# Narrow TensorE products placed among wide ones in a hybrid decoder block

## The reference, cut to what matters

```python
mod = (silu(c) @ ada_w + ada_b).reshape(B, 6, D)       # shift1, scale1, gate1, shift2, scale2, gate2
h = rms_norm(x, norm1_g) * (1 + scale1) + shift1
u = h @ w_in          # g_q, g_k, g_v, g_r, g_lr (16 wide, low rank), d_q, d_k, d_v, gate_a, gate_b
log_a = log_sigmoid(g_lr @ alpha_up + alpha_b) / 16    # per token, 4 heads x 64
# GLA in chunks of 64 tokens, for each chunk:
b = cumsum(log_a)                                      # forward sums
q_in, k_in = q * exp(b), k * exp(-b)
k_out = k * exp(b_last - b)                            # sums to the chunk's end
decay = exp(b_last)                                    # one number per chunk and channel: chunk sums
o_b = diff_attention(...)                              # d_q, d_k, d_v
x = x + gate1 * ((sig(gate_a) * (o_a @ w_a) + sig(gate_b) * (o_b @ w_b)) @ w_out)
h2 = rms_norm(x, norm2_g) * (1 + scale2) + shift2
x = x + gate2 * moe(h2)
```

## Time and profile before

| | |
|---|---|
| median of 3 runs | 1588.11 us (1584.22 to 1591.04) |
| profiled execution, its own time | 1586.0 us |
| its span, first to last instruction | 1584.2 us |
| TensorE busy | 1501.9 us, 95% of the span |
| VectorE, ScalarE, GpSimd busy | 520.9, 342.0 and 106.5 us |
| mean granted TensorE clock | 0.977 of full speed |

### The profile page before, as it was taken

The page is one execution under the profiler, slowest core; times in us unless marked ns, Lnnn a source line. Parts: engine busy times, 40 slices in busy tenths (PEclk is TensorE's granted clock), DMA queues, the critical chain, the costliest instruction groups (busy, mean ns, idle before and its releaser), DMA issues.

```text
span 1584.2 us, 20243 instructions
## 1 busy us (share of the span) xinstructions
PE 1501.9 (95%) x7989; PEld 675.8 (43%) x7989; DVE 520.9 (33%) x1074; ACT 342.0 (22%) x662; POOL 106.5 (7%) x140
## 2 busy tenths in 40 slices
PE   2999999999999999999999999889999899989896
PEld 2444545454545555444444455433333233323232
DVE  6576332323233224732222344652111111111010
ACT  4312322323233614211111112211101101101010
POOL 1000000000000000000000001001111111111101
PEclk9999999999999999999999999989999999999999
DMA  9760101010101011011130752469999999999982
GB/s 373 277 263 12 50 0 54 1 47 6 26 13 27 13 27 27 27 40 40 40 119 0 305 185 94 178 249 345 410 408 406 410 409 409 408 414 407 417 360 54
DMA packets 68748, 291.23 MB, mean 184 GB/s; under 512 B 12180, under 2 KB 36927, under 8 KB 53311
## 3 DMA queue, kind: packets, MB, share of 16 engines
q1 hardware_dynamic: 62096, 273.38, 43.5%
q0 software_dynamic: 6576, 16.79, 4.2%
HBM read 276.36 MB, written 20.07 MB: 187 GB/s over the span
## 4 chain that ended last, share of the span: by engine, by line
PE 86%; DMA 11%; DVE 2%; issue 1%; ACT 1%; SPq 0%; POOL 0%; POOLq 0%; ACTq 0%; DVEq 0%
PE PS L676 81%; DMA WK<-in_expert_w 5%; DMA R<-in_expert_w 3%; DMA R<-in_ada_w 1%; DMA out_rows<-R 1%; PE PS L1119 1%; PE PS L784 1%; PE PS L1141 1%; DVE R L1526 1%; PE PS L745 0%; ACT R L1216 0%; PE PS L1039 0%; PE PS L897 0%; DMA R<-in_x 0%; DVE R L1518 0%
## 5 line engine op out<-in xcount | busy, mean ns | idle before, releaser
L676 PE MATMUL PS<-R 128*32 128x512 f32 (+5 forms) x4058 | 747.1, 578 | 23.7 <-DMA R<-in_expert_w 7.5
L676 PEld LDWEIGHTS PS<-R 128*32 128x32 f32 (+4 forms) x4058 | 262.7, 129 | 396.8 <-issue 381.6
L676 PE MATMUL PS<-R,HT 128*128 128x512 f32 (+1 forms) x768 | 341.1, 599 | 3.7 <-DVE HT L1523 3.0
L676 PE MATMUL PS<-HT,R 128*32 128x512 f32 (+2 forms) x1184 | 314.4, 602 | 3.5 <-DMA WK<-in_expert_w 1.9
L1518 DVE TENSOR_TENSOR R<-R,PS 128x512 f32<-128x512 f32 (+1 forms) x95 | 71.6, 771 | 464.1 <-PE PS L676 464.1
L676 PEld LDWEIGHTS PS<-R,HT 128*128 128x128 f32 x768 | 143.9, 192 | 169.5 <-issue 168.1
L676 PEld LDWEIGHTS PS<-HT,R 128*32 128x32 f32 (+1 forms) x1184 | 105.8, 133 | 145.9 <-issue 143.1
L1216 ACT ACTIVATE R<-PS 128x512 f32<-128x512 f32 (+4 forms) x129 | 76.8, 605 | 396.9 <-PE PS L676 252.7
L676 PE MATMUL PS<-WK,R 128*32 128x512 f32 (+1 forms) x384 | 95.2, 614 | 4.5 <-DMA R<-in_expert_w 4.5
L640 POOL DMA_INDIRECT out_rows<-R x37 | 53.6, 1448 | 309.1 <-DVE R L1526 172.8
L1216 ACT ACTIVATE R<-PS,S,A 128x128 f32<-128x128 f32 x88 | 33.1, 456 | 189.5 <-PE PS L1119 189.5
(11 more groups left out here) (239 smaller groups left out, 831.4 us busy)
## 6 DMA issues: line engine op xcount, KB each, us to landing
R<-in_expert_w SPq DMA_DIRECT2D x67, 2048.0 KB, 34.9
HT<-in_expert_w SPq DMA_DIRECT2D x20, 2048.0 KB, 32.8
R<-in_ada_w SPq DMA_DIRECT2D x24, 1024.0 KB, 7.4
WK<-in_expert_w SPq DMA_DIRECT2D x9, 2048.0 KB, 36.6
R<-in_w_in SPq DMA_DIRECT2D x6, 2048.0 KB, 7.9
R<-in_w_in SPq DMA_DIRECT2D x16, 512.0 KB, 4.6
R<-in_x SPq DMA_DIRECT2D x2, 2048.0 KB, 13.6
R<-in_x SPq DMA_DIRECT2D x8, 512.0 KB, 3.7
```

The costliest lines, as they stand in the source:

```text
L676: return nc.tensor.matmul(o, l, r, start=a, stop=z)
```

## The change

In the first place the 16 narrow products no longer stand in a row. The wait for the last projection tile's copy (`proj_free`) moves ahead of them, and each of eight steps now issues one wide product of the low-rank projection and two narrow ones, one of each conditioning vector. `glr_mm` and `mods_ps` are both raised at the end of the mixed row.

In the second place the chunk sums go to bank 6 instead of bank 4 and are issued four at a time, after each turn and forward sum. The sums to the end come in the order 3, 2, 0, 1, one after each of turns 4 and 5, and two at the end. ScalarE takes the exponential of the chunk sums between its fourth and its fifth copy of the attention output.

```diff
             e.wait_ge(s["proj_free"], NT + NT + 1)
+            def glr(half, k):
+                return mm(bank(1 + 2 * half)[0:RANK, :], wlr[:, k, :], hT[:, k, half * 512:(half + 1) * 512],
+                          k == 0, k == KT - 1)
+
+            e.wait_ge(s["proj_free"], 4 + 2 * NT)
             for j in range(KT):
+                low_rank = glr(0, j)
                 mm(bank(0)[:, j:j + 1], acc[:, 1, 1024 + j:2048:KT], onesf[:, 0:1])
-            for j in range(KT):
                 last = mm(bank(0)[:, 8 + j:9 + j], acc[:, 2, j:1024:KT], onesf[:, 0:1])
+            low_rank.then_inc(s["glr_mm"], 1)
             last.then_inc(s["mods_ps"], 1)
-
-            def glr(half):
-                for k in range(KT):
-                    last = mm(bank(1 + 2 * half)[0:RANK, :], wlr[:, k, :], hT[:, k, half * 512:(half + 1) * 512],
-                              k == 0, k == KT - 1)
-                last.then_inc(s["glr_mm"], 1)
-
-            e.wait_ge(s["proj_free"], 4 + 2 * NT)
-            glr(0)
             e.wait_ge(s["gates_done"], 1)
...
-            glr(1)
+            for k in range(KT):
+                last = glr(1, k)
+            last.then_inc(s["glr_mm"], 1)
...
             for b in range(4):
                 turn_ob(b)
                 last = mm(bank(b), tri[:, :], sp[:, 512 * b:512 * (b + 1)])
+                if b == 0:
+                    e.wait_ge(s["early_sig"], 1)
+                for x in range(4 * b, 4 * b + 4):
+                    chunk = mm(bank(6)[:, 2 * x:2 * x + 2], sp[:, x * P:(x + 1) * P], blk[:, 0:P:CH])
             last.then_inc(s["cum_mm"], 1)
+            chunk.then_inc(s["dec_mm"], 1)
+            turn_ob(4)
             e.wait_ge(s["early_sig"], 2)
-            for b in (2, 3):
-                turn_ob(2 + b)
-                last = sums_to_end(b)
-            last.then_inc(s["cum_mm"], 1)
+            sums_to_end(3)
+            turn_ob(5)
+            e.wait_ge(s["dec_done"], 1)
+            sums_to_end(2).then_inc(s["cum_mm"], 1)
             turn_ob(6)
             turn_ob(7)
             e.wait_ge(s["obT_done"], 7)
-            for t in range(NT):
-                for pr in range(2):
-                    last = mm(bank(4)[:, t * 4 + pr * 2:t * 4 + pr * 2 + 2],
-                              sp[:, t * 256 + pr * P:t * 256 + (pr + 1) * P], blk[:, 0:P:CH])
-            last.then_inc(s["dec_mm"], 1)
+            sums_to_end(0)
             e.wait_ge(s["obT_done"], NT)
-            sums_to_end(1)
-            e.wait_ge(s["dec_done"], 1)
-            sums_to_end(0).then_inc(s["cum_mm"], 1)
+            sums_to_end(1).then_inc(s["cum_mm"], 1)
             e.wait_ge(s["eb_done"], 1)
...
-            for t in range(NT):
+            def ob_turned(t):
                 e.wait_ge(s["ob_tr"], t + 1)
                 act(obT[:, :, t * P:(t + 1) * P], bank(4 + t % 2).rearrange("p (h t) -> p h t", h=NH),
                     ACT.Copy, scale=gcols[:, 19:20]).then_inc(s["obT_done"], 1)
+
+            for t in range(4):
+                ob_turned(t)
+            e.wait_ge(s["dec_mm"], 1)
+            act(dec[:, :], bank(6)[:, 0:4 * NT], ACT.Exp).then_inc(s["dec_done"], 1)
+            for t in range(4, NT):
+                ob_turned(t)
             e.wait_ge(s["cum_mm"], 2)
             e.wait_ge(s["gv_moved"], 1)
             act(R2[:, 7168:8192], bank(6, 2), ACT.Exp).then_inc(s["eb_done"], 1)
-            e.wait_ge(s["dec_mm"], 1)
-            act(dec[:, :], bank(4)[:, 0:4 * NT], ACT.Exp).then_inc(s["dec_done"], 1)
             act(R2[:, 2048:4096], bank(0, 4), ACT.Exp).then_inc(s["eb_done"], 1)
```

## The result

The changed kernel takes 1590.74 us in the median of 20 runs (1586.43 to 1597.28), the kernel before 1586.86 us in 20 runs (1582.13 to 1591.12). The ratio is 1.0028, with a 95% interval from 1.0017 to 1.0040: some 4 us slower, within the half per cent that I had called no change, but clear of noise and against a forecast of 3.3 us less. The single profiled execution took 1594.96 us, 4.2 above its median, and its mean granted clock, 0.971, is the lowest that any of the 20 shows (0.971 to 0.978). So its span of 1593.1 us is not all the change's doing.

The account below looks back on a forecast made before the run. TensorE was taken to bound the kernel (86% of the chain). First place +0.4 and second -3.7 gave -3.3 us: 1582.7 on the profiled execution, 1584.8 in the median 2.1 above it, range 1579.5 to 1591.0.

Parts of the forecast that it names:

- The cost of a narrow product in a row: Both places: the weight load is paid, not the columns; 0.233 us each in the first, 0.11 in the second.
- The step that failed first: First place: one of four narrow loads hides under the second wide instruction, three stay exposed; a step takes 1.64 us.
- The step that failed second: First place: the mixed row keeps full clock, eight steps take 13.1 us; avoiding the old fall is worth 2.2.
- rival (b): Mixed rows lose the clock; first place alone: row 19.9 us, place +5.7, time 1590.1 or 1591.7; chance 0.11.
- The gates' wait: First place: TensorE stands still 2.3 us before the turns, as ScalarE's gate copies wait for the mixed row's end.
- The fall with it: First place: the clock falls after the gates' wait and slows the turns by 1.5 us, somewhat likelier than not.
- The second place: Attention's turns to gates: blocks of 2.1 us, no wait for `dec_done`, gates start at full clock; -3.7 us.
- The 1 to 1 count: Whole kernel: a microsecond taken from either place moves everything behind it by about a microsecond.
- Rival (d): Expert stage: what is gained ahead is waited for there, so nothing moves; 1588 us, chance 0.07.
- Rival (c): Weight loads cheaper in the mix (-6.3, 1581.8) or all hidden in both places (-12, 1576); chance 0.08.
- Rival (b) in the second place: Mixed blocks lose the clock: +3.7 in place of -3.7; alone 1592.2, chance 0.03; with first place about 1598, 0.06.
- The range: Whole time: 1579.5 to 1591.0 us, from the mild end of (c) to (b) in the first place.

Follow-up runs that it names:

- the run alone: Only the second place changed, the first left as in the kernel before: 1582.35 us, ratio 0.9969 (0.9953 to 0.9985).

## Why the prediction was wrong

**The cost of a narrow product in a row** was read rightly: the weight load is paid and not the columns, and the strided load costs twice the adjacent one (0.26 against 0.135 us in the mixed row). In the mixed row it is a little dearer than the 0.233 that I took over.

**The step that failed first** is "the first narrow load lies under the second wide instruction". In the second place it does, with weights of 128 columns on both sides (the load starts at 540.02 in the changed kernel, 0.42 us ahead of its matmul); in the first it did not, and all four loads were exposed, 0.26 us each. 2.00 us a step instead of 1.64 is 2.9 us over eight steps; 0.26 of the 0.36 is the load that did not hide, the rest the dearer loads. Giving the wide product 128 columns brought the step to 1.68. That kernel also takes its weights from another tensor and fills all rows of the bank, so by itself it does not single out the column count; the load at 175.23 in the kernel before, behind the unaltered row with 16 columns, points the same way. That load could have warned me: I read only the timeline of matmuls there and carried the habit of the other rows over without a bound for it.

**The step that failed second** is the clock in the first place, rival (b) there. All four profiles with steps of 2.00 us lost it (after 4, 4, 4.3 and 12 us), both with steps of 1.68 us kept it, and so did the single ones with 1.50 us and with one wide product to each narrow one, which have 16 columns as well. So it goes with the exposed loads, which thinned the row: the first failure most likely caused the second. The profiles are few, and one row of 2.00 us steps held for 12 us. Rival (b) had priced it at 19.9 us for the row, +5.7 to +7.3 in the first place and +2.0 to +3.6 us in all, with a chance of 0.11. Measured were 21.1 and 17.4 us for the row in two profiles of the changed kernel (158.60 to 179.7, 160.52 to 177.9), +8.8 and +4.6 us for the place, and +3.9 us between the medians. The mechanism was named. That the price fits is partly luck: it had 2.49 us for a step at half clock, where 2.86 were measured, and it had the clock down from the start, where it held for two steps or six. Its chance was too small, since the load that would not hide and the thin mix are one risk and not two.

**The gates' wait** was right: 2.3 us predicted, 2.16 of idle time measured, and gone with a counter of its own. **The fall with it** came in the run with wide weights (1.3 us on the turns, 1.5 predicted, though 3.4 us at half clock would by my own rule cost 1.7) and did not in the one with adjacent columns; one profile each, so chance, as in the forecast, is not told from the mix. In the changed kernel the clock was down already.

**The second place** was right in each step: blocks of 2.1 us, no wait for `dec_done`, full clock, 21.2 us against 24.8, so -3.6 where I had -3.7. The wait for the seventh copy was 0.34 us, not 0.6. Its worth varies with the kernel before, which took 23.1 to 24.8 us there in the profiles with the old order, by where its clock fell. In the times of the run alone it is 4.9 us (2.4 to 7.5).

**The 1 to 1 count** holds. The end of the first early gate lies between 548.1 and 563.2 us in the 13 profiles of kernels whose results are comparable, and from there to the end of the span all of them take 1028.8 to 1032.7 us. Rival (d) falls.

**Rival (c)** falls in both forms: no load became cheaper or hid beyond the first, except where the columns were made adjacent. The load of 128 columns took 0.135 or 0.26 us in the mixed row by their stride. Nor did a second load go under the same matmul: in the second place the first narrow load ran for 0.19 us from 540.02, and the next one started at 540.45, with the first narrow matmul.

**Rival (b) in the second place** falls too: the blocks, a third of whose wide work is transposes, kept their 2.1 us and a clock of 1.00 in all four kernels that have them. And in the first place of the changed kernel the clock came back under nothing but turns (0.54 from 182 to 187, 1.00 from 187 to 190).

**The range** held: the median of 1590.74 lies inside 1579.5 to 1591.0, near its edge. What was wrong is the sign, by the failure above.

## What to carry to other kernels

Before narrow products are spread among wide ones, look in the timeline of loads for whether the narrow weight load really starts under the wide matmul. With 128 stationary columns in the wide product it did here, and the place took 21.4 us with the gates apart; with 16 it did not, and the place took 30.4, against 24.4 in the old order. One semaphore raised at the end of a mixed row holds back every reader of either product (2.16 us of waiting here); give work that is ready earlier its own counter. In the changed kernel TensorE was busy for all of the 4.00 us ahead of the fall and all of the 16.07 us behind it, which ran at a clock of 0.50, so a mix has to be read by its granted clock, in more than one execution.

## What the hardware showed beyond expectation

A load of 128 stationary columns did not start under a matmul whose own weights had 16 columns (start at 159.56, at its end, and at 175.23 in the kernel before), and did under one with 128 (159.08, half-way). The other order did not hide either: the 16-column load behind a matmul with 128 started at its end (158.60). It is only cheap, 0.11 us for two, which is why a wide product takes 0.96 us in the mixed row and not 0.86.

A strided load of 128 f32 columns (every 8th) took 0.23 to 0.26 us at either clock level (0.28 with one narrow product to each wide one). An adjacent one took 0.11 to 0.135 us at a granted clock of 1.00 and some 0.18 at 0.50.

The clock's falls differ from one execution of the same kernel to the next in time and number: the unchanged kernel's three profiles had 17.5, 17.5 and 20.8 us for the same products between the places, and the changed kernel's two lost the clock after 4 and after 12 us of the same row. This scatter alone is worth several microseconds, as much as the change.
